# MLP down-projection of a two-block layer: a third pair by seven products, and half of the ordinary low parts made by ScalarE and an accumulating GpSimd transfer

## The chip, the core and the metric

The program runs on one core of one Trainium2 chip. The metric is device time in microseconds; the median of three runs is shown. The engines are named as in the profile: PE is TensorE's matrix multiplication and PEld its weight load, DVE is VectorE, ACT is ScalarE, POOL is GpSimd, SP is SyncE, which issues the loads.

## What is computed

The reference is a pair of transformer blocks on 256 tokens of width 2048. The first block ends with an MLP, and that is the part the change touches:

```python
u = jax.nn.relu(rms_norm(h, mlp_norm_g) @ w_up)      # 256 x 8192
h = h + (u * u) @ w_down                             # 8192 x 2048
```

All is float32. The projections before it (attention mixers) and the second block after it are left as they are.

## The kernel before

**Products in three terms.** Every float32 product is made of two `float32r` parts. The weights arrive from HBM as `raw`; ACT copies them to `w_high` (line 1274), which rounds; DVE makes `w_low = raw - w_high` (line 1593). The activations have a high and a low part too. PE adds high x high, high x low and low x high, so each product is three matmuls of 512 columns (lines 957, 958 and 959 in the quad jobs).

**Windows.** The weights of all projections come as one stream of 884 windows of 128 x 1024 (512 KB). There are `RAW_SLOTS` = 6 slots of `raw` and `AHEAD` = 5 slots of `w_high` and `w_low`. While PE works on window w, ACT and DVE split window w + 5. Every engine walks the same list (`walk`, line 552): window w, then the early stages of w, then the split of w + 5, then the late stages. ACT's split of s waits for the load of s and for `window_done` of s - 5, because its slot is still read until then. DVE's split waits for ACT's and for the same window. SP's `load(w)` (line 770) waits until the split of w - 6 has left its slot of `raw`. DVE counts its splits in `low_ready`, and PE waits for that count before each window.

**The MLP.** `plan_mlp` (line 344) runs four blocks of 2048 hidden features. A block has eight `features` jobs of four windows each (u = x W_up, transposed, with wide matmuls at line 970 and narrow ones at 982), then two `quads` jobs for W_down, each of which makes 1024 of the 2048 output columns; the fourth block has one quad job and two `tokens` jobs instead. That is seven quad jobs. A stage `u_square`, `u_split` squares and splits the hidden features of every second job (j = 0 to 3) into `actB`.

**A quad job** (`QuadJob`, line 87) goes through eight pairs of 128-row chunks in `QUAD_ORDER`. An "eight" pair takes two windows (side 0 and side 1), each with four products, 12 matmuls, so 24 in all. A "seven" pair multiplies its 2 x 2 blocks by Winograd's form of Strassen's scheme with seven products, 21 matmuls: its parts 0, 1 and 2 hold two products each (6 matmuls) and part 3 holds one (3 matmuls). Parts 0 and 1 are loaded; parts 2 and 3 hold sums of the weights that DVE makes in the free slots of `raw` (`sums_of`, lines 1603 to 1606). The matching sums of the activations ("forms") are made once per block by the stage `u_forms`: four sums on DVE, the high part on ACT (line 1476), the low part on DVE (line 1899). Before the change the sevens are pairs 0 and 1, so a quad job has 20 windows and 186 matmuls.

**Taking results away.** After the last seven, `add_sevens` (ACT line 1481, DVE lines 1912 to 1919) combines the seven products into H; after the job, `add_quads` (line 1929) adds the rest. The sevens use the banks of the other buffer, so a seven of one job waits for `add_quads` of the job before.

**GpSimd** makes only a few square roots by a power (lines 842, 846, 852) and issues no transfer. Below, k0, k1, ... are the windows of one quad job.

Of the kernel before, what the change touches and what calls it, by code (L numbers as in the profile page):

```python
# [16 lines left out]
P = 128  # L17
T = 256
# [490 lines left out]


SUMS = list(itertools.accumulate(int(part_of(w) == 1) for w in range(PLAN.windows)))

# [93 lines left out]
def build(nc, d, out):  # L606
    ctx = ExitStack()
    with ctx:
# [3 lines left out]
        def sem(name):  # L612
            return ctx.enter_context(nc.semaphore(name))
# [6 lines left out]
        act_high, act_low = ({n: act_both[n][:, :, part, :] for n in "AB"} for part in (0, 1))  # L620
        forms_both = sb("forms_both", [P, 2, 1024], F32R)
        H = sb("H", [P, TT, D])
# [68 lines left out]

        forms, forms_high, forms_low = m_slot(0), forms_both[:, 0, :], forms_both[:, 1, :]
        form_at = lambda f, p: slice(((f - 1) * 2 + SEVENS.index(p)) * P, ((f - 1) * 2 + SEVENS.index(p) + 1) * P)
        p1, u_one, u_two = slots[:, 4, 0:COLS], slots[:, 4, COLS:2 * COLS], slots[:, 5, 0:COLS]
# [26 lines left out]
        act_self, dve_self = sem("act_self"), sem("dve_self")  # L721
        sums_made = sem("sums_made")
        out_ready, half_done, wide_done = sem("out_ready"), sem("half_done"), sem("wide_done")
# [41 lines left out]
        def _(sp):  # L765
# [61 lines left out]
        def _(pool):  # L827
# [5 lines left out]
            def stage(w, name, *a):  # L833
# [13 lines left out]
                elif name in ("head_norm", "o_norm", "post_stat"):  # L847
# [5 lines left out]
                                            ALU.pow).then_inc(S["rstd"], 1)  # L853
            walk(n, lambda w: None, lambda w, s: None, stage)

        @block.tensor
        def _(pe):
# [65 lines left out]
            def products(w, tokens):  # L923
# [4 lines left out]
                if w > 0:  # L928
                    pe.wait_ge(low_ready, w + 1)
                for cc, c in enumerate(chunks_of(w)):  # L930
# [13 lines left out]
            def quads(w):  # L944
                job, k = WINDOW[w]
                first_of(w)
                pe.wait_ge(low_ready, w + 1)
                for x, (bank, (of, i, where), cc) in enumerate(job.products(k)):
                    cols = slice(cc * COLS, (cc + 1) * COLS)
                    if of == "u":  # L950
                        once("u_low", 4 * job.needs[1] + i // 4 + 1)
                        ah, al = (a["B"][:, i, where * P:(where + 1) * P] for a in (act_high, act_low))
                    else:
                        once("forms_low", job.needs[1] + 1)
                        ah, al = (a[:, form_at(i, where)] for a in (forms_high, forms_low))
# [19 lines left out]
            def narrow(w):  # L975
                job, k = WINDOW[w]
                ends = k == job.windows - 1
                pe.wait_ge(low_ready, w + 1)
                for cc, c in enumerate(chunks_of(w)):
# [266 lines left out]
        def _(act):  # L1246
# [8 lines left out]
            def split(w, s):  # L1255
# [12 lines left out]
                if s >= AHEAD and WINDOW[s - AHEAD][0].kind == "features":  # L1268
                    act.wait_ge(low_ready, s - AHEAD + 1)
                    act.wait_ge(wide_done, WIDE[s - AHEAD])  # L1270
                elif s >= AHEAD:
                    act.wait_ge(window_done, s - AHEAD + 1)
                cols = slice(0, COLS if part_of(s) == 3 else 2 * COLS)
                nc.scalar.activation(w_high[:, s % AHEAD, cols], raw[:, s % RAW_SLOTS, cols], ACT.Copy)\  # L1274
                    .then_inc(high_ready, 1)

            as_att = lambda: att[:, 2:4, :]

            def stage(w, name, *a):
# [193 lines left out]
                elif name == "u_forms":  # L1473
                    wait(act, n, "forms_made")
                    wait(act, n, "h_added", 0)
                    nc.scalar.activation(forms_high, forms, ACT.Copy).then_inc(S["forms_high"], 1)
                elif name == "add_sevens":
# [92 lines left out]
        def _(dve):  # L1570
# [8 lines left out]
            def split(w, s):  # L1579
                if s == 0:  # L1580
                    for half_, made, signal in ((slice(0, COLS), first_high, first_low),
# [14 lines left out]
            def sums_of(s):  # L1596
# [33 lines left out]
            def stage(w, name, *a):  # L1630
# [255 lines left out]
                elif name == "u_forms":  # L1886

                    wait(dve, n, "u_squared", 0)
                    wait(dve, n, "forms_high", 0)
                    u = a_slot(2).rearrange("p (q c x t) -> p q c x t", q=2, c=2, x=TT)  # L1890
                    a11, a12, a21, a22 = (u[:, :, c, x, :] for x, c in ((0, 0), (0, 1), (1, 0), (1, 1)))
                    s1, s2, s3, s4 = (forms[:, i * T:(i + 1) * T].rearrange("p (q t) -> p q t", q=2) for i in range(4))
                    done(nc.vector.tensor_tensor(s1, a21, a22, ALU.add))
# [4 lines left out]
                    wait(dve, n, "forms_high")  # L1898
                    nc.vector.tensor_tensor(forms_low, forms, forms_high.bitcast(F32), ALU.subtract)\
                        .then_inc(S["forms_low"], 1)  # L1900
# [269 lines left out]
```

## Time and profile before

| | us |
|---|---|
| median of 3 runs | 2503.59 (2503.17 to 2504.42) |
| span of the profiled execution | 2504.0 |
| PE busy | 2480.6 |
| DVE busy | 1753.6 |
| ACT busy | 1257.8 |
| POOL busy | 29.5 |

The profiled execution is given by its span alone, from its first instruction to its last; it lies 0.4 us above the median of the runs, so the span is taken as its time. Busy time counts the instructions' own durations. Matmuls overlap: a row of one 128 x 512 matmul reads 0.39 us, but the next one starts earlier than that, so the distance between starts is what counts. An instruction's idle time is followed by what released it.

### The profile page before, as it was taken

To read this page: it belongs to the slowest core of one execution; us is meant where nothing else is said; L and a number is where in the kernel's file an instruction comes from. 1 tells how busy PE (TensorE), PEld (TensorE's weight loads), DVE (VectorE), ACT (ScalarE), POOL (GpSimd) and SP (SyncE) were. 2 spreads that over 40 slices of the span, in tenths; PEclk is the share of its full clock that TensorE was granted. 3 is DMA by queue.
4 is the path that set the end of the run, shared out by engine and by line. 5 is a ranking of instruction groups with operands and counts; after the bars stand their busy time and mean duration, and the time that the engine had idled before them with its cause. 6 is when DMAs were issued, how large, how long until landed. Compare 5 with 4: busy or idle time off the path is not lost.

```text
span 2504.0 us, 38061 instructions
## 1 busy us (share of the span) xinstructions
PE 2480.6 (99%) x15416; PEld 2115.6 (84%) x15416; DVE 1753.6 (70%) x1978; ACT 1257.8 (50%) x1506; POOL 29.5 (1%) x26
## 2 busy tenths in 40 slices
PE   9999999999999999999999999999999999999998
PEld 7888888888888888888888888888888888888886
DVE  6656765668668677675777777775776666777777
ACT  7655344544444444445555555544654444444543
POOL 0000000000000000000000000000000000000000
PEclk9999999999999999999999999999999999999999
DMA  9454545546546546555545454556465565556553
GB/s 381 153 183 152 176 153 193 176 164 223 193 161 231 187 171 211 193 195 183 185 153 185 153 185 153 185 170 195 150 217 185 186 200 187 183 194 198 186 188 127
DMA packets 128239, 465.97 MB, mean 186 GB/s; under 512 B 14368, under 2 KB 14624, under 8 KB 127168
## 3 DMA queue, kind: packets, MB, share of 16 engines
q1 hardware_dynamic: 127920, 463.53, 55.2%
q8 instruction: 122, 2.00, 0.3%
q14 instruction: 53, 0.43, 0.1%
q10 hardware_dynamic: 144, 0.02, 0.0%
HBM read 461.39 MB, written 2.10 MB: 185 GB/s over the span
## 4 chain that ended last, share of the span: by engine, by line
PE 94%; issue 4%; DVE 2%; ACT 0%; DMA 0%; SPq 0%; DVEq 0%; POOL 0%; POOLq 0%
PE job L970 30%; PE job L982 16%; PE job L938 11%; PE job L940 11%; PE job L939 11%; PE job L957 2%; PE job L958 2%; PE job L959 2%; PE att L958 2%; PE att L957 2%; PE att L959 2%; PE att L1177 1%; PE att L998 0%; DVE w_low L1593 0%; PE att L1010 0%
## 5 line engine op out<-in xcount | busy, mean ns | idle before, releaser
L1274 ACT ACTIVATE w_high<-raw 128x1024 fp32r<-128x1024 f32 (+1 forms) x883 | 919.6, 1050 | 733.9 <-PE job L940 292.4
L1593 DVE TENSOR_TENSOR w_low<-raw,w_high 128x1024 fp32r<-128x1024 f32 (+1 forms) x883 | 1047.0, 1212 | 310.5 <-ACT w_high L1274 231.0
L970 PE MATMUL job<-actA,w_high 128*128 128x512 f32 x3328 | 798.3, 391 | 0.1
L970 PEld LDWEIGHTS job<-actA,w_high 128*128 128x128 f32 x3328 | 611.8, 188 | 119.9 <-issue 0.7
L982 PEld LDWEIGHTS job<-actA,w_low 128*128 128x128 f32 x3328 | 426.7, 191 | 16.2
L982 PE MATMUL job<-actA,w_low 128*128 128x256 f32 x3328 | 431.7, 283 | 0.0
L1796 DVE TENSOR_TENSOR slots<-job,slots 128x512 f32<-128x512 f32 x102 | 70.5, 691 | 344.1 <-ACT slots L1466 343.5
L938 PE MATMUL job<-w_high,actB 128*128 128x512 f32 x736 | 288.6, 392 | 2.5 <-DVE w_low L1593 2.0
L939 PE MATMUL job<-w_low,actB 128*128 128x512 f32 x736 | 287.1, 390 | 0.0
L940 PE MATMUL job<-w_high,actB 128*128 128x512 f32 x736 | 287.0, 390 | 0.0
L938 PE MATMUL job<-w_high,actA 128*128 128x512 f32 x576 | 230.9, 401 | 0.0
L940 PE MATMUL job<-w_high,actA 128*128 128x512 f32 x576 | 224.8, 390 | 0.0
L939 PE MATMUL job<-w_low,actA 128*128 128x512 f32 x576 | 224.6, 390 | 0.0
L1466 ACT ACTIVATE slots<-job 128x512 f32<-128x512 f32 x102 | 61.0, 598 | 240.6 <-PE job L982 240.6
L938 PEld LDWEIGHTS job<-w_high,actB 128*128 128x128 f32 x736 | 138.5, 188 | 32.2 <-DVE w_low L1593 2.4
L940 PEld LDWEIGHTS job<-w_high,actB 128*128 128x128 f32 x736 | 138.5, 188 | 28.9
L939 PEld LDWEIGHTS job<-w_low,actB 128*128 128x128 f32 x736 | 138.7, 188 | 28.1
L940 PEld LDWEIGHTS job<-w_high,actA 128*128 128x128 f32 x576 | 108.1, 188 | 23.4
L938 PEld LDWEIGHTS job<-w_high,actA 128*128 128x128 f32 x576 | 108.1, 188 | 22.7
L939 PEld LDWEIGHTS job<-w_low,actA 128*128 128x128 f32 x576 | 108.2, 188 | 21.1
L957 PE MATMUL job<-w_high,actB 128*128 128x512 f32 x210 | 82.2, 392 | 2.1 <-DVE w_low L1593 2.1
L958 PE MATMUL job<-w_low,actB 128*128 128x512 f32 x210 | 81.8, 390 | 0.0
(257 smaller groups left out, 1906.0 us busy)
## 6 DMA issues: line engine op xcount, KB each, us to landing
raw<-in_weights SPq DMA_DIRECT2D x855, 512.0 KB, 4.2
M<-in_mem_t SPq DMA_DIRECT2D x8, 256.0 KB, 8.0
slots<-in_mem SPq DMA_DIRECT2D x2, 1024.0 KB, 12.2
M<-in_x_t SPq DMA_DIRECT2D x4, 512.0 KB, 13.8
H<-in_x SPq DMA_DIRECT2D x2, 1024.0 KB, 9.0
out<-H SPq DMA_DIRECT2D x8, 256.0 KB, 3.2
slots<-in_w_small SPq DMA_DIRECT2D x1, 1024.0 KB, 9.7
slots<-in_post_mix_g SPq DMA_DIRECT2D x1, 1024.0 KB, 4.3
```

The costliest lines, as they stand in the source:

```text
L938: nc.tensor.matmul(to, ah, w_high[:, slot, cols], start=begins and cc == 0, stop=False)
L939: nc.tensor.matmul(to, ah, w_low[:, slot, cols], start=False, stop=False)
L940: mm = nc.tensor.matmul(to, al, w_high[:, slot, cols], start=False, stop=ends and cc == job.per - 1)
L957: nc.tensor.matmul(to, ah, w_high[:, w % AHEAD, cols], start=(k, x) in job.firsts, stop=False)
L958: nc.tensor.matmul(to, ah, w_low[:, w % AHEAD, cols], start=False, stop=False)
L959: mm = nc.tensor.matmul(to, al, w_high[:, w % AHEAD, cols], start=False, stop=(k, x) in job.lasts)
L970: mm = nc.tensor.matmul(J[job.buf][:, x, :], w_high[:, w % AHEAD, cols], act_both[job.act][:, c, :, :].rearrange("p a t -> p (a t)"), star ...
L982: mm = nc.tensor.matmul(J[job.buf][:, x, T:2 * T], w_low[:, w % AHEAD, cols], act_high[job.act][:, c, :], start=False, stop=ends and cc == ...
L1274: nc.scalar.activation(w_high[:, s % AHEAD, cols], raw[:, s % RAW_SLOTS, cols], ACT.Copy)\
L1466: nc.scalar.activation(by_feature(JOIN[to][:, half_ * COLS:(half_ + 1) * COLS]), J[buf][:, :, T:2 * T], ACT.Copy).then_inc(S["low_copied"], 1)
L1593: nc.vector.tensor_tensor(w_low[:, s % AHEAD, cols], raw[:, s % RAW_SLOTS, cols], w_high[:, s % AHEAD, cols].bitcast(F32), ALU.subtract).t ...
L1796: nc.vector.tensor_tensor(x, J[buf][:, :, 0:T], x, ALU.add).then_inc(S["joined"], 1)
```

## The change

The third seven: `QUAD_ORDER` makes pairs 0, 1 and 2 sevens, in another order. A quad job now has 22 windows: k0, k1 an eight, k2 to k5 a seven, k6, k7 an eight, k8 to k11 a seven, k12, k13 an eight, k14 to k17 a seven, and two eights in k18 to k21. `forms_both` grows from 1024 to 1536 columns, and `u_forms` runs for j = 0 (pairs 0 and 1, as before) and for j = 1 (pair 2, half the width).

The low parts: `by_transfer(w)` holds for side 1 of an eight whose slot was not used last by a `features` window. For such a window DVE makes no low part. ACT writes `-w_high` into the slot of `w_low` with a second copy of `raw` by -1, and POOL, which waits for that, issues a transfer of the same 512 KB of weights from HBM that is added to the slot. PE waits for the transfer's semaphore. It holds for k7, k13, k19 and k21 in every quad job, and for k1 too where the job before was a quad job: 4 x 4 + 3 x 5 = 31 transfers. All waits on `low_ready` are recounted, and SP and `sums_of` wait for ACT's second copy where there is no low part by DVE.

```diff
-QUAD_ORDER = (("eight", 2), ("seven", 0), ("eight", 3), ("eight", 4), ("seven", 1), ("eight", 5), ("eight", 6), ("eight", 7))
+QUAD_ORDER = (("eight", 3), ("seven", 0), ("eight", 4), ("seven", 1), ("eight", 5), ("seven", 2), ("eight", 6), ("eight", 7))
...
-            if j == 0:
-                p.put(job.end + 2, "u_forms", b)
+            if j < 2:
+                p.put(job.end + 2, "u_forms", j)
...
+def by_transfer(w):
+
+    job, k = WINDOW[w]
+    return (job.kind == "quads" and job.parts[k][0] == "eight" and job.parts[k][2] == 1
+            and WINDOW[w - AHEAD][0].kind != "features")
...
+        def low_wait(engine, w):
+
+            if by_transfer(w):
+                engine.wait_ge(low_landed[w % AHEAD], 16 * LANDED[w])
+            else:
+                engine.wait_ge(low_ready, LOWS[w])
+
+        def raw_wait(engine, w):
+
+            if by_transfer(w):
+                engine.wait_ge(neg_made, NEGS[w])
+            else:
+                engine.wait_ge(low_ready, LOWS[w])
...
-                    sp.wait_ge(low_ready, w - RAW_SLOTS + 1 + (part_of(w - RAW_SLOTS) == 0))
+                    raw_wait(sp, w - RAW_SLOTS + (part_of(w - RAW_SLOTS) == 0))
...
+            def split(w, s):
+
+                if by_transfer(s):
+                    pool.wait_ge(neg_made, NEGS[s])
+                    nc.gpsimd.dma_start(w_low[:, s % AHEAD, :], d["weights"][LOAD_AT[s] - 1], accum_op=ALU.add)\
+                        .then_inc(low_landed[s % AHEAD], 16)
+
+            walk(n, lambda w: None, split, stage)
...
                 nc.scalar.activation(w_high[:, s % AHEAD, cols], raw[:, s % RAW_SLOTS, cols], ACT.Copy)\
                     .then_inc(high_ready, 1)
+                if by_transfer(s):
+                    nc.scalar.activation(w_low[:, s % AHEAD, :], raw[:, s % RAW_SLOTS, :], ACT.Copy, scale=-1.0)\
+                        .then_inc(neg_made, 1)
...
+                if by_transfer(s):
+                    return
                 if part_of(s) == 1:
                     sums_of(s)
...
-                dve.wait_ge(low_ready, s + 3 - RAW_SLOTS)
+                raw_wait(dve, s + 1 - RAW_SLOTS)
+                raw_wait(dve, s + 2 - RAW_SLOTS)
```

## Rows read from the trace of the kernel before

**Rows 1.** The page: busy time of the engines, and the chain that ended last.
```profile
PE 2480.6 (99%) x15416; PEld 2115.6 (84%) x15416; DVE 1753.6 (70%) x1978; ACT 1257.8 (50%) x1506; POOL 29.5 (1%) x26
...
PE 94%; issue 4%; DVE 2%; ACT 0%; DMA 0%; SPq 0%; DVEq 0%; POOL 0%; POOLq 0%
```

**Rows 2.** Two stretches by windows: one quad job each, columns as headed.
```profile
core 0: us, PE busy (x) PEld busy (x) DVE busy (x) ACT busy (x) POOL busy (x), PEclk, DMA share, GB/s
...
550.71:594.30 43.59, 42.55 (x188) 34.57 (x186) 38.36 (x43) 21.54 (x23) 0.00 (x0) 1.00 0.54 193
...
594.30:636.60 42.30, 42.30 (x188) 35.05 (x187) 34.47 (x38) 21.46 (x22) 0.00 (x0) 1.00 0.64 224
```

**Rows 3.** Timeline of PE in the second quad job: start us, us, engine, line.
```profile
594.53 0.39 PE L957 MATMUL job<-w_high,actB 128*128 128x512 f32 x1
...
595.21 0.39 PE L957 MATMUL job<-w_high,actB 128*128 128x512 f32 x1
...
599.97 0.39 PE L957 MATMUL job<-w_high,actB 128*128 128x512 f32 x1
...
601.33 0.39 PE L957 MATMUL att<-w_high,forms_both 128*128 128x512 f32 x1
...
607.45 0.39 PE L957 MATMUL att<-w_high,actB 128*128 128x512 f32 x1
...
636.69 3.79 PE L970 MATMUL job<-actA,w_high 128*128 128x512 f32 x16
```

**Rows 4.** Waits of the whole span: who for whom, us, times, longest.
```profile
PEld job L957 <- DVE w_low L1593: 7.5, 8, 1.0
...
PE job L957 <- DVE w_low L1593: 4.1, 8, 0.5
```

**Rows 5.** Timeline of the first quad job: start us, us, engine, line.
```profile
558.40 1.06 ACT L1471 ACTIVATE actB<-slots 128x1024 fp32r<-128x1024 f32 x1 [0.96 <-DVE slots L1878]
...
558.67 0.39 PE L959 MATMUL att<-w_high,forms_both 128*128 128x512 f32 x1
...
559.37 5.02 ACT L1274 ACTIVATE w_high<-raw 128x1024 fp32r<-128x1024 f32 x5
...
559.56 0.50 PE L957 MATMUL job<-w_high,forms_both 128*128 128x512 f32 x1 [0.51 <-DVE w_low L1593]
...
561.16 5.76 DVE L1593 TENSOR_TENSOR w_low<-raw,w_high 128x1024 fp32r<-128x1024 f32 x5
...
562.43 0.50 PE L957 MATMUL job<-w_high,actB 128*128 128x512 f32 x1 [0.53 <-DVE w_low L1593]
```

**Rows 6.** Timeline of ACT in the second quad job: start us, us, engine, line.
```profile
601.59 1.06 ACT L1274 ACTIVATE w_high<-raw 128x1024 fp32r<-128x1024 f32 x1 [0.30 <-PE job L959]
...
602.95 1.06 ACT L1274 ACTIVATE w_high<-raw 128x1024 fp32r<-128x1024 f32 x1 [0.30 <-PE att L959]
...
604.30 2.01 ACT L1274 ACTIVATE w_high<-raw 128x1024 fp32r<-128x1024 f32 x2 [0.30 <-PE att L959]
```

**Rows 7.** Line 776 from 550 to 637 us: issues on SP, and to landing.
```profile
L776 SPq DMA_DIRECT2D raw<-in_weights x36: 327/328/433, 557.3 to 636.6; - x36
...
DMA to landing us min/median/max: 3.1/4.5/6.8
```

**Rows 8.** Line 852: duration ns min/median/max of a POOL instruction.
```profile
L852 POOL TENSOR_TENSOR rstd<-msq,half x13: 695/1637/2552, 60.4 to 1755.7; 128x8 f32<-128x8 f32 x12, 128x2 f32<-128x2 f32 x1
```

**Rows 9.** The page: GB/s that the DMA engines moved, 40 slices.
```profile
GB/s 381 153 183 152 176 153 193 176 164 223 193 161 231 187 171 211 193 195 183 185 153 185 153 185 153 185 170 195 150 217 185 186 200 187 183 194 198 186 188 127
```

**Rows 10.** Groups of DVE, 540 to 1125 us: busy us, mean ns, idle.
```profile
L1593 DVE TENSOR_TENSOR w_low<-raw,w_high 128x1024 fp32r<-128x1024 f32 x229 | 272.7, 1221 | 56.1 <-ACT w_high L1274 36.7 <-PE job L982 15.4
...
L1604 DVE TENSOR_TENSOR raw<-raw 128x512 f32<-128x512 f32 x14 | 9.7, 692 | 0.5
...
L1899 DVE TENSOR_TENSOR forms_both<-M,forms_both 128x1024 fp32r<-128x1024 f32 x3 | 3.7, 1225 | 3.6 <-ACT forms_both L1476 3.6
```

**Rows 11.** Wait of ACT for the forms, 480 to 550 us.
```profile
ACT forms_both L1476 <- DVE M L1896: 3.1, 1, 3.1
```

More of the change, by code:

```diff
@@ L508, in part_of @@
     return job.parts[k][2] if job.kind == "quads" and job.parts[k][0] == "seven" else None
+def by_transfer(w):
+    job, k = WINDOW[w]
+    return (job.kind == "quads" and job.parts[k][0] == "eight" and job.parts[k][2] == 1
+            and WINDOW[w - AHEAD][0].kind != "features")
+LOWS = list(itertools.accumulate(int(not by_transfer(w)) for w in range(PLAN.windows)))
+NEGS = list(itertools.accumulate(int(by_transfer(w)) for w in range(PLAN.windows)))
+LANDED = [sum(by_transfer(v) for v in range(w % AHEAD, w + 1, AHEAD)) for w in range(PLAN.windows)]
 SUMS = list(itertools.accumulate(int(part_of(w) == 1) for w in range(PLAN.windows)))
@@ L620, in build @@
         act_high, act_low = ({n: act_both[n][:, :, part, :] for n in "AB"} for part in (0, 1))
-        forms_both = sb("forms_both", [P, 2, 1024], F32R)
+        forms_both = sb("forms_both", [P, 2, 1536], F32R)
         H = sb("H", [P, TT, D])
@@ L690, in build, with form_at @@
         post_g = a2(6)
-        forms, forms_high, forms_low = m_slot(0), forms_both[:, 0, :], forms_both[:, 1, :]
-        form_at = lambda f, p: slice(((f - 1) * 2 + SEVENS.index(p)) * P, ((f - 1) * 2 + SEVENS.index(p) + 1) * P)
+        forms, forms_high, forms_low = Mf[:, 0:1536], forms_both[:, 0, :], forms_both[:, 1, :]
+        form_cols = lambda j: slice(0, 1024) if j == 0 else slice(1024, 1536)
+        def form_at(f, p):
+            at = (f - 1) * 2 * P + SEVENS.index(p) * P if p < 2 else 1024 + (f - 1) * P
+            return slice(at, at + P)
         p1, u_one, u_two = slots[:, 4, 0:COLS], slots[:, 4, COLS:2 * COLS], slots[:, 5, 0:COLS]
@@ L722, in build @@
         sums_made = sem("sums_made")
+        neg_made, low_landed = sem("neg_made"), [sem(f"low_landed{i}") for i in range(AHEAD)]
         out_ready, half_done, wide_done = sem("out_ready"), sem("half_done"), sem("wide_done")
@@ L928, in products @@
                 if w > 0:
-                    pe.wait_ge(low_ready, w + 1)
+                    low_wait(pe, w)
                 for cc, c in enumerate(chunks_of(w)):
@@ L946, in quads @@
                 first_of(w)
-                pe.wait_ge(low_ready, w + 1)
+                low_wait(pe, w)
                 for x, (bank, (of, i, where), cc) in enumerate(job.products(k)):
@@ L953, in quads @@
                     else:
-                        once("forms_low", job.needs[1] + 1)
+                        once("forms_low", 2 * job.needs[1] + (1 if where < 2 else 2))
                         ah, al = (a[:, form_at(i, where)] for a in (forms_high, forms_low))
@@ L977, in narrow @@
                 ends = k == job.windows - 1
-                pe.wait_ge(low_ready, w + 1)
+                low_wait(pe, w)
                 for cc, c in enumerate(chunks_of(w)):
@@ L1268, in split @@
                 if s >= AHEAD and WINDOW[s - AHEAD][0].kind == "features":
-                    act.wait_ge(low_ready, s - AHEAD + 1)
+                    act.wait_ge(low_ready, LOWS[s - AHEAD])
                     act.wait_ge(wide_done, WIDE[s - AHEAD])
@@ L1475, in stage @@
                     wait(act, n, "h_added", 0)
-                    nc.scalar.activation(forms_high, forms, ACT.Copy).then_inc(S["forms_high"], 1)
+                    cols = form_cols(a[0])
+                    nc.scalar.activation(forms_high[:, cols], forms[:, cols], ACT.Copy).then_inc(S["forms_high"], 1)
                 elif name == "add_sevens":
@@ L1889, in stage @@
                     wait(dve, n, "forms_high", 0)
-                    u = a_slot(2).rearrange("p (q c x t) -> p q c x t", q=2, c=2, x=TT)
+                    j, pairs = a[0], 2 - a[0]
+                    u = a_slot(2 + j).rearrange("p (q c x t) -> p q c x t", q=2, c=2, x=TT)[:, 0:pairs]
                     a11, a12, a21, a22 = (u[:, :, c, x, :] for x, c in ((0, 0), (0, 1), (1, 0), (1, 1)))
-                    s1, s2, s3, s4 = (forms[:, i * T:(i + 1) * T].rearrange("p (q t) -> p q t", q=2) for i in range(4))
+                    s1, s2, s3, s4 = (forms[:, form_cols(j)].rearrange("p (f q t) -> p f q t", f=4, q=pairs)[:, f]
+                                      for f in range(4))
                     done(nc.vector.tensor_tensor(s1, a21, a22, ALU.add))
@@ L1898, in stage @@
                     wait(dve, n, "forms_high")
-                    nc.vector.tensor_tensor(forms_low, forms, forms_high.bitcast(F32), ALU.subtract)\
+                    cols = form_cols(j)
+                    nc.vector.tensor_tensor(forms_low[:, cols], forms[:, cols], forms_high[:, cols].bitcast(F32),
+                                            ALU.subtract)\
                         .then_inc(S["forms_low"], 1)
```

1 line of the change is left out of this document (removed).

## The prediction

> **What bounds the kernel now.** I read the page first. PE is busy 99% of the span and holds 94% of the chain that ended last, so time falls only where PE has less to do or waits less, and it rises with every wait put before a matmul [rows 1]. Next, the windows of two quad jobs. In the second PE is busy all 42.30 us; in the first 42.55 of 43.59. DVE is busy 38.36 and 34.47 us there, near its limit, while ACT has half its time free (21.5 us busy) and POOL is idle [rows 2]. The third view is PE's timeline. Three matmuls take 595.21 - 594.53 = 0.68 us, 0.227 us each; the whole job goes from 594.53 to 636.69, 42.16 us, which is 186 x 0.227 [rows 3]. So a full window is 2.72 us, parts 0 to 2 of a seven 1.36 us, part 3 0.68 us. The waits come last: DVE's low part is late eight times in the span [rows 4], two each in the four quad jobs that follow features. One is 559.56 - 558.67 - 0.227 = 0.66 us [rows 5]; eight make 5.3 us.
>
> **The change part by part.** *The third seven.* It replaces 24 matmuls by 21 in seven jobs: 21 x 0.227 = 4.8 us off PE, all on the path. This is the whole gain that arithmetic gives, 0.19% of the span.
>
> *DVE.* An eight costs it two low parts, 2 x 1.22 = 2.4 us; a seven three and a half of them and four sums of 0.69 us, 3.5 x 1.22 + 4 x 0.69 = 7.0 us [rows 10]. The third seven adds 4.6 us a job; the four or five low parts given away take 4.9 to 6.1 off. If DVE kept them, a first job would want 43.0 us of DVE in about as much of PE; so it keeps its load of today. Giving them away removes a wait that the third seven would bring, and none that is there now: the two late low parts of a first job hang on `u_square` and `u_split`, which stay in their place ahead of k4 and k6. I take zero, and 5.3 us as the most that could come.
>
> *The forms.* The second `u_forms` is half as wide as the first, whose four sums keep ACT waiting 3.1 us [rows 11] before ACT's copy of 1.06 us and DVE's low part of 1.22 us [rows 10]; at most 5.4 us in each of four blocks. It stands in the features jobs, where the first one makes PE wait for nothing: none of PE's waits for DVE names it [rows 4]. Cost zero; with no cover at all it would be 4 x 5.4 = 22 us.
>
> *The deadline of the sums.* The second seven now starts at k8, right after a seven and one eight. Counted from the start of k4, DVE gets there by ACT's copy (0.26 + 1.06), the low part of k8 (1.22), four sums (2.8), a copy and a low part (2.5): 7.8 us. PE is at k9 after 1.36 + 0.68 + 2.72 + 2.72 + 1.36 = 8.84 us. The slack is 1.0 us (4.4 before). The loads of k14 and k15 wait for the low part of k9 and land at about the time they are needed; a load at the slow end of 6.8 us [rows 7] would be late by some 1.2 us. I take zero, because a stall at k7 or k13, below, gives just this slack back; the bound is 2 x 7 x 1.2 = 17 us.
>
> *The traffic.* Each job has 16 loads as before, and five transfers more, whose bytes are read from HBM and whose target is read too. By bytes this is at most 5 x 2 x 0.524 MB in 42 us, 125 GB/s on top of 224 [rows 2]; together 349, and the first slice shows 381 [rows 9]. So bandwidth does not stop it, but loads and transfers share the same engines and stretch each other.
>
> *The transfer, on which it all hangs.* ACT's copy of a window begins 0.26 us after PE starts the window that follows the freeing one, because it needs `window_done`. In the second job k3 starts at 601.33 and ACT copies k7 from 601.59 [rows 3, 6]. Two copies back to back take 2.01 us [rows 6], so -w_high stands at 603.60. PE wants k7 at 607.45 [rows 3]. **The transfer has 3.85 us** from POOL's wait to its semaphore. For k13 and k19 the four windows between are the same (1.36 + 1.36 + 0.68 + 2.72 = 6.12 us), so is the allowance. For k21 the windows between are 8.84 us long, which gives 6.6 us plus the stall of k19, and for k1 four full ones, 10.9 us, which gives 8.6; these two I cost at nothing, whatever the latency below.
>
> In the four jobs after features k7 is tighter. ACT waits there until 558.40 for `u_split` and then copies k6, k7, ... from 559.37, 1.0 us each [rows 5]; the third copy in this chain would be -w_high of k7, done at 562.41. PE wants k7 at 562.43 + 2.72 = 565.15 [rows 5]: 2.74 us.
>
> Let L be the time from POOL's release to landing. PE stalls L - 3.85 at 17 places (three in each of seven jobs, less the four) and L - 2.74 at four: together 21 L - 76.4 us, as long as L is over 3.85. A stall is not made good later: the next deadline is counted from PE's own windows, which move along. With the 4.8 us off, the change costs **21 L - 81.2 us**; it breaks even at L = 3.87 us and is slower by 0.2% (5 us, about what a measurement here can tell) at 4.1 us.
>
> No accumulating transfer and none issued by POOL is in this trace. The nearest rows are SP's loads of the same 512 KB in this stage: 3.1 us at the least, 4.5 the median, 6.8 the most, and 0.33 us of issuing [rows 7]. The low end is L = 3.1, where adding and POOL's issuing cost nothing. For the high end I add to the slowest load a second pass for reading the target, 0.524 MB at 381 GB/s = 1.4 us, and POOL's slowest instruction, 2.55 us [rows 8]: 10.8 us. I take the median load and one second pass, 4.5 + 1.4 = **5.9 us**, nearest to the middle row because the transfer meets a load in flight most of the time (36 loads of 4.5 us in 79 us). The stalls are then 17 x 2.05 + 4 x 3.16 = 47.5 us.
>
> The Trainium skill, page "DMA: Bandwidth & Descriptors", section "Anatomy of one DMA", puts a GpSimd-issued transfer at about 2.0 us plus bytes over 436 GB/s. By that estimate L is 3.2 us, only k7 of the first jobs is late (4 x 0.46), and the sum would be 2504.0 - 4.8 + 1.8 = 2501.0 us; it prices no adding and no other traffic, and no row here has such a transfer.
>
> **Sum.** 2504.0 - 4.8 + 47.5 = 2546.7 us on the profiled execution. Its span is 0.4 us above the median, so against the median of the runs 2546.3; I say 2546.
>
> **The rivals.** *The transfer fits (20%).* Place: between ACT's second copy and PE's wait before k7, k13 and k19. If adding is done in the stream and costs no second pass, and POOL issues as fast as SP, L is near the 3.1 us of the fastest load, 17 stalls vanish and four of 0.36 us stay: 2504.0 - 4.8 + 1.4 - 0.4 = 2500 us, not slower. It decides from L below 3.87, and stays within 0.2% up to 4.1. For it: the loads of 3.1 us. Against it: half of all loads already take over 4.5.
>
> *No second pass, but the crowd (10%).* L = 4.5: 21 x 4.5 - 81.2 = 13 us, 2517 us.
>
> *A slow issue (18%).* POOL writes out its transfer in software and takes as long as its slowest instruction, 2.55 us, on top of 5.9: L = 8.4, 21 x 8.4 - 81.2 = 95 us, 2599 us. For it: POOL's eight columns take 1.64 us in the median [rows 8]. Or POOL has to wait out a low part of DVE, 1.22 us, when it wants the memory port: L = 7.1, 2572 us. The Trainium skill, page "SBUF — State Buffer", section "Who interferes with whom", says that a DVE instruction with two SBUF inputs holds up only GpSimd's reads; by this rule the latter does not happen. No run shows it yet.
>
> *The late low parts vanish too (6%).* If DVE's relief reached k4 and k6 of the first jobs and the transfers fit, 2504.0 - 4.8 - 5.3 - 0.4 = 2493.5 us. Against it: those low parts are late behind work that the change leaves in place.
>
> **How the numbers follow.** The forecast, L between 4.9 and 6.9, gets 46%, and 2546 is its value. Slower by over 0.2%: 46 + 10 + 18 = 74%; within 0.2%: 20%; faster: 6%. The range goes from 2500 (the transfer fits) to 2594 (L = 8.2, the slowest load with a second pass: 21 x 8.2 - 81.2 = 91 us, less the 0.4); it leaves out the 6% below and about half of the slow case above.
>
> **What would show it.** Right: PE has 15395 matmuls, 21 fewer. In the chain and the waits, PE waits for a transfer into `w_low` 21 times, some 2 us each at k13 and k19, some 3 us at k7 of the first jobs; ACT has 31 copies by -1, DVE 24 fewer 1024-column low parts (31 given away, 14 fewer eights' and 21 more sevens') and 28 more sums; from POOL's issue to landing the median is near 5.9 us. At k1 and k21 there is no wait. Wrong: a median under 4 us with a PE that never waits for it, or waits that name DVE's low parts at k9 and k15, which would mean that the sums and not the transfers are late.

## The result, and the profile after

The change makes the kernel slower: 2645.13 us, median of five runs (2643.86 to 2646.54), against 2503.75 us for the kernel before in the same session. The ratio is 1.0563, with a 95% interval of 1.0551 to 1.0576. I had forecast 2546 us, with a range up to 2594: the direction was right, the size was not, by 99 us, and the time lies 51 us outside the range. In the table of experiments one of four runs of transfers_only is left out: it took 3103.9 us at a granted clock of 0.749, in a slow state of the chip.

The page of the kernel after, from its parts 1, 2 (TensorE's granted clock), 4, 5 and 6; it answers to [rows 1]:

```profile
span 2643.2 us, 38150 instructions
PE 2529.9 (96%) x15395; PEld 2145.4 (81%) x15395; DVE 1756.5 (66%) x2009; ACT 1296.5 (49%) x1555; POOL 56.8 (2%) x57
PEclk9999999988998898898999999999999999999999
PE 87%; DMA 6%; issue 3%; ACT 2%; DVE 0%; SPq 0%; DVEq 0%; POOL 0%; ACTq 0%; POOLq 0%
L995 PE MATMUL att<-w_high,actB 128*128 128x512 f32 x140 | 76.5, 546 | 90.1 <-DMA w_low<-in_weights 90.1
w_low<-in_weights POOLq DMA_DIRECT2D x31, 512.0 KB, 7.8
```

The granted clock on the page of the kernel before:

```profile
PEclk9999999999999999999999999999999999999999
```

Two things are new. The chain that ended last now has a DMA in it, 6% of the span, and its group says which: the transfer into `w_low`. And in the row of the clock, slices 9 to 19 read 8 in seven places, where before every slice read 9. The quad jobs lie there. PE's busy time also rose, by 49.3 us, although it has 21 matmuls less; an engine that does less work in more busy time is working more slowly. The mean of L995's `att` matmuls, 546 ns where one of these takes 390 otherwise, says the same.

The waits of the kernel after for the new transfer, over the whole span, then DVE's late low parts from 540 to 1300 us, and POOL's issues with the time from issue to landing; they answer to [rows 4, 7]:

```profile
PEld att L995 <- DMA w_low<-in_weights: 99.0, 21, 5.8
PE att L995 <- DMA w_low<-in_weights: 90.1, 21, 5.4
...
PE job L995 <- DVE w_low L1637: 4.2, 8, 0.5
...
L889 POOL DMA_DIRECT2D w_low<-in_weights x31: 872/872/1063, 560.9 to 1242.9; - x31
...
DMA to landing us min/median/max: 6.4/7.8/10.6
```

PE waits at the 21 places foretold and nowhere else for a transfer. DVE's eight late low parts are there as before. But a transfer takes 7.8 us in the median, not 5.9.

The timeline of the kernel after, from ACT's copy to the end of the first late window, k7 of the first quad job; it answers to [rows 5]:

```profile
559.55 1.04 ACT L1315 ACTIVATE w_low<-raw 128x1024 fp32r<-128x1024 f32 x1
560.91 1.06 POOL L889 DMA_DIRECT2D w_low<-in_weights  x1 [91.58 <-ACT w_low L1315]
563.34 0.39 PE L997 MATMUL job<-w_high,actB 128*128 128x512 f32 x1
569.13 0.79 PE L995 MATMUL att<-w_high,actB 128*128 128x512 f32 x1 [5.40 <-DMA w_low<-in_weights]
569.73 0.63 PE L996 MATMUL att<-w_low,actB 128*128 128x512 f32 x1
570.15 0.63 PE L997 MATMUL att<-w_high,actB 128*128 128x512 f32 x1
...
573.90 0.39 PE L997 MATMUL att<-w_high,actB 128*128 128x512 f32 x1
```

The same stretch by windows (us, PE, PEld, DVE, ACT and POOL busy with their counts, granted clock, DMA share, GB/s):

```profile
564.00:570.00 6.00, 0.87 (x2) 0.77 (x3) 4.38 (x6) 2.52 (x3) 0.00 (x0) 0.75 0.90 213
570.00:574.00 4.00, 4.00 (x11) 3.08 (x11) 0.00 (x0) 0.00 (x0) 0.00 (x0) 0.53 0.43 170
574.00:578.00 4.00, 4.00 (x20) 3.29 (x19) 1.22 (x1) 3.30 (x4) 0.00 (x0) 1.00 0.11 15
```

PE idles 5.40 us. Then matmuls start 0.427 us apart, not 0.227: the granted clock is 0.53, close to the half that is the 1.2 GHz level, while PE is busy all the time. At 573.9 it is back at 2.4 GHz. From 569.13 to 573.90 there are 11 starts in 4.77 us; at full clock they take 2.50. So this one wait costs 5.40 us, and 2.27 us more behind it.

**Where the 139.2 us of span went** (2643.2 - 2504.0). The 21 matmuls give back 4.8. The waits are 90.1, and each costs 0.16 more from start to start, because a row's 0.39 us ends later than the next matmul would have begun (0.39 - 0.227): 93.5 together. That leaves 139.2 + 4.8 - 93.5 = 50.5 us, 2.4 for each wait. I also added up, from the starts of the matmuls after each wait, what they take over 0.227 us apiece: 52 us, 1.7 to 3.0 behind each of the 21. The slow clock is the rest. (In runs the difference is 141.4; the other 2 us are that the page of before lay 0.4 us above its median, while this span lies 1.9 below.)

The fall doesn't always come at once. A later wait of the kernel after:

```profile
630.71 0.50 PE L995 MATMUL att<-w_high,actB 128*128 128x512 f32 x1 [4.19 <-DMA w_low<-in_weights]
631.05 0.40 PE L996 MATMUL att<-w_low,actB 128*128 128x512 f32 x1
...
632.12 0.63 PE L997 MATMUL att<-w_high,actB 128*128 128x512 f32 x1
```

Here PE works over a microsecond at full clock before it slows down. Someone who looks only at the first matmul after a wait misses it.

### The profile page after: what moved, and what is told of

Read it like the earlier page. It is cut to its first block, busy times and chain, and to the rows that moved or that the text cites. A ratio compares the mean times of both kernels' runs of the same rounds, so it can differ in the third digit from the quotient of the medians.

```text
span 2643.2 us, 38150 instructions
## 1 busy us (share of the span) xinstructions
PE 2529.9 (96%) x15395; PEld 2145.4 (81%) x15395; DVE 1756.5 (66%) x2009; ACT 1296.5 (49%) x1555; POOL 56.8 (2%) x57
## 4 chain that ended last, share of the span: by engine, by line
PE 87%; DMA 6%; issue 3%; ACT 2%; DVE 0%; SPq 0%; DVEq 0%; POOL 0%; ACTq 0%; POOLq 0%
PE job L1008 29%; PE job L1020 15%; PE job L976 11%; PE job L978 10%; PE job L977 10%; DMA w_low<-in_weights 6%; PE att L995 2%; PE att L996 2%; PE att L997 2%; ACT w_high L1312 1%; PE job L995 1%; PE job L996 1%; PE job L997 1%; ACT w_low L1315 1%; PE att L1215 1%
## 5 line engine op out<-in xcount | busy, mean ns | idle before, releaser
L1637 DVE TENSOR_TENSOR w_low<-raw,w_high 128x1024 fp32r<-128x1024 f32 (+1 forms) x866 | 1024.6, 1208 | 445.0 <-ACT w_high L1312 370.3
L976 PE MATMUL job<-w_high,actB 128*128 128x512 f32 x736 | 287.9, 391 | 2.3 <-DVE w_low L1637 1.5
L977 PE MATMUL job<-w_low,actB 128*128 128x512 f32 x736 | 286.6, 389 | 0.0
L978 PE MATMUL job<-w_high,actB 128*128 128x512 f32 x736 | 286.4, 389 | 0.0
L995 PE MATMUL att<-w_high,actB 128*128 128x512 f32 x140 | 76.5, 546 | 90.1 <-DMA w_low<-in_weights 90.1
L995 PEld LDWEIGHTS att<-w_high,actB 128*128 128x128 f32 x140 | 36.3, 260 | 107.0 <-DMA w_low<-in_weights 99.0
## 6 DMA issues: line engine op xcount, KB each, us to landing
slots<-in_w_small SPq DMA_DIRECT2D x1, 1024.0 KB, 10.4
```

The costliest lines, as they stand in the source:

```text
L976: nc.tensor.matmul(to, ah, w_high[:, slot, cols], start=begins and cc == 0, stop=False)
L977: nc.tensor.matmul(to, ah, w_low[:, slot, cols], start=False, stop=False)
L978: mm = nc.tensor.matmul(to, al, w_high[:, slot, cols], start=False, stop=ends and cc == job.per - 1)
L995: nc.tensor.matmul(to, ah, w_high[:, w % AHEAD, cols], start=(k, x) in job.firsts, stop=False)
L1637: nc.vector.tensor_tensor(w_low[:, s % AHEAD, cols], raw[:, s % RAW_SLOTS, cols], w_high[:, s % AHEAD, cols].bitcast(F32), ALU.subtract).t ...
```

## Experiments

**What is to be told apart.** My theory now: the latency of the transfer sets the 21 waits, and each wait then costs a stretch at half clock. Rivals: the third seven or its forms cost PE something of their own; the slow matmuls come from something else, such as the transfers' traffic; and the latency is made by adding, by POOL's issuing, by bytes or by the loads beside it.

| kernel | median us (runs) | ratio to before, 95% | granted clock |
|---|---|---|---|
| after | 2645.13 (5) | 1.0563 [1.0551, 1.0576] | 0.972 |
| sevens_only | 2522.33 (5) | 1.0077 [1.0064, 1.0090] | 0.995 |
| transfers_only | 2579.26 (3) | 1.0293 [1.0277, 1.0309] | 0.990 |
| wait_filled | 2599.68 (4) | 1.0383 [1.0367, 1.0399] | 0.997 |
| high_first | 2589.25 (4) | 1.0340 [1.0324, 1.0356] | 0.986 |
| plain_from_pool | 2587.53 (1) | - | 0.987 |
| half_transfer | 2594.04 (1) | - | 0.985 |
| thin_loads | 2583.08 (1) | - | 0.985 |
| before_high_first | 2497.84 (9) | 0.9975 [0.9966, 0.9985] | 0.997 |
| long_lead_high_first | 2526.12 (4) | 1.0087 [1.0073, 1.0101] | 0.996 |
| one_lead_high_first | 2519.52 (5) | 1.0062 [1.0049, 1.0074] | 0.995 |
| sevens_high_first | 2522.39 (5) | 1.0073 [1.0060, 1.0087] | 0.993 |
| later_first_seven | 2513.48 (5) | 1.0039 [1.0026, 1.0053] | 0.997 |

Kernels with one run are compared by their profiles, and their time only roughly. These three leave out part of the low parts or of the weights, so their results are wrong; they serve to measure times alone.

### The two halves of the change: sevens_only, transfers_only

```diff
# sevens_only, in by_transfer: DVE makes every low part
-            and WINDOW[w - AHEAD][0].kind != "features")
+            and WINDOW[w - AHEAD][0].kind != "features" and False)
# transfers_only: two sevens, the order of before
-QUAD_ORDER = (("eight", 3), ("seven", 0), ("eight", 4), ("seven", 1), ("eight", 5), ("seven", 2), ("eight", 6), ("eight", 7))
+QUAD_ORDER = (("eight", 2), ("seven", 0), ("eight", 3), ("eight", 4), ("seven", 1), ("eight", 5), ("eight", 6), ("eight", 7))
```

> The change with no transfer at all: three sevens in the new order, every low part by DVE. If the whole loss of the change lies in the transfers (my theory: 21 waits of 4 to 6 us and the slower clock after each), this is near 2504 - 4.8 = 2499 us, 2498 to 2508 with a late low part here and there. Rival, the third seven needs the relief (DVE has 43.0 us of work in 43.1 us of PE, and the second and third seven leave 1.0 us for their sums): then PE waits for DVE at k9 and k15, by 1 to 3 us each, and the time is 2510 to 2540 us.

> The change with the order of before: two sevens, transfers kept. They now fall on k1 (second jobs), k7, k9, k15, k17 and k19. Between a window five back and its use lie 6.12 us at k7 and k15, but 8.84 us at k9 and k17 and 10.9 us at k19. My theory (the stall is the latency less the room the windows leave) expects waits at k7 and k15 only, 14 of them, of 4 to 6 us, some 1.3 us or less at k9 and k17, and about 2504 + 14 x (4.3 + 2.2) = 2595 us. Rival (any transfer stalls PE, because POOL, the queue or the port is the trouble): waits at all of k7, k9, k15, k17, k19, and over 2640 us.

Waits of sevens_only, 540 to 1300 us, and `add_quads` and two matmuls at its longest wait:

```profile
PE job L995 <- DVE H L1978: 11.2, 3, 4.1
PE job L995 <- DVE w_low L1637: 5.3, 9, 1.1
...
601.21 1.40 DVE L1978 SCALAR_TENSOR_TENSOR H<-job,rstd,H 128x512 f32<-128x512 f32 x2
602.53 1.40 DVE L1978 SCALAR_TENSOR_TENSOR H<-att,rstd,H 128x512 f32<-128x512 f32 x2
603.98 0.80 PE L995 MATMUL job<-w_high,actB 128*128 128x512 f32 x1 [4.10 <-DVE H L1978]
604.58 0.63 PE L996 MATMUL job<-w_low,actB 128*128 128x512 f32 x1
```

The third seven alone makes the kernel 18 us slower although it has 21 matmuls less. The time is the rival's, the place is neither's: at k9 and k15 PE waits next to nothing. It waits at k2 of three second jobs for `add_quads` of the job before (line 1978), and these waits too are followed by slow matmuls (some 1.7 us lost behind each). The third seven ends four windows before the end of the job instead of six, so `add_sevens`, some 6 us of DVE, is done later, the low parts and sums stand behind it, and `add_quads` behind them. In the kernel after this wait is absent. The low parts given away have made room on DVE, but PE's own stalls, 13 us a job, also give DVE time, and this run does not part the two. Whatever share is the transfers', they cost more than it.

Waits of transfers_only over the whole span:

```profile
PE att L995 <- DMA w_low<-in_weights: 47.2, 17, 4.6
```

It waits at k7 and k15 of the seven jobs (14) and a little at three k9. The places are those of my theory, and not the rival's; the time is 16 us under the 2595 us foretold, because the seven waits at k7 are 1.7 to 2.7 us long instead of 4 to 6. Its clock is 0.990: the third seven isn't needed for the slow stretches. Waits of 0.8 to 1.8 us were followed by less than 0.2 us of loss, those of 3.9 to 4.6 us by 1.6 to 3.0 (from the starts of the matmuls, as above); between them it varied. A wait of 1.94 us was followed by 1.7 us of loss, one of 3.56 us by 0.1.

### The clock: wait_filled, high_first

```diff
# wait_filled: four matmuls of zeros, added to the bank in use, ahead of the wait
+                if by_transfer(w) and k in (7, 13, 19):
+                    pe.wait_ge(zeros_set, 1)
+                    for _ in range(4):
+                        nc.tensor.matmul(quad_bank(job.buf, ("C", 1, 0)), zeros[:, 0:P], zeros,
+                                         start=False, stop=False)
                 low_wait(pe, w)
```

> The change, with four float32 matmuls of zeros (128 x 512, added to a bank of the job, which they leave as it is) put ahead of PE's wait at k7, k13 and k19. The transfers and their latency are as in the change. Theory: the clock falls because PE stands still for about 4 us, and that costs 2.4 us after each of 21 waits, 50 us in all. With the wait filled the granted clock stays at 1.0 and the time is about 2643 - 50 = 2593 us, a little more where the zeros run past the landing. Rival: the clock falls for another reason, and the time stays at 2645 us with rows of 0.63 us after the wait.

Windows of wait_filled, the first two of the stretch shown above, and its timeline there (the profile has two records for each of the four float32 matmuls of zeros, hence x8):

```profile
564.00:570.00 6.00, 3.73 (x10) 1.62 (x9) 4.42 (x6) 2.52 (x3) 0.00 (x0) 1.00 0.89 212
570.00:574.00 4.00, 4.00 (x19) 3.25 (x19) 0.29 (x1) 1.09 (x2) 0.00 (x0) 1.00 0.42 171
...
563.62 3.60 PE L989 MATMUL att<-slots 128*128 128x512 f32 x8
569.48 0.50 PE L1001 MATMUL att<-w_high,actB 128*128 128x512 f32 x1 [2.27 <-DMA w_low<-in_weights]
569.81 0.40 PE L1002 MATMUL att<-w_low,actB 128*128 128x512 f32 x1
```

This run settles what makes the matmuls slow. The first late window begins at 569.48 (569.13 in the kernel after), so the transfer is no earlier; the DMA engines are as busy (0.89 and 0.90, then 0.42 and 0.43). Only PE's idle time is cut, from 5.40 to 2.27 us, by work that is worth nothing. The clock stays at 1.00, 19 matmuls start in the next 4 us instead of 11, and the span is 47.3 us shorter. That is nearly the 50 us from above, found by another way. The traffic of the transfers is not the cause.

```diff
# high_first: in a transfer's window the terms with w_high come before the wait
-                low_wait(pe, w)
+                later, high_first = [], by_transfer(w)
+                if high_first:
+                    pe.wait_ge(high_ready, w + 1)
+                else:
+                    low_wait(pe, w)
...
+                    if high_first:
+                        nc.tensor.matmul(to, al, w_high[:, w % AHEAD, cols], start=False, stop=False)
+                        later.append((to, ah, cols, (k, x) in job.lasts))
+                        continue
...
+                if high_first:
+                    low_wait(pe, w)
+                    for to, ah, cols, last in later:
+                        mm = nc.tensor.matmul(to, ah, w_low[:, w % AHEAD, cols], start=False, stop=last)
```

> The change, but in a window that takes its low part from a transfer PE first does the eight matmuls that need w_high alone and waits for the transfer only then. 8 x 0.227 = 1.8 us of each wait is covered: 21 x 1.8 = 38 us less, 2607 us, if the clock falls after a wait of 2.5 to 4 us as after one of 4.3 to 5.8. If the shorter waits leave the clock at its upper level, another 21 x 2.2 = 46 us comes back: 2561 us.

Waits of high_first, 540 to 1300 us:

```profile
PE att L1009 <- DMA w_low<-in_weights: 56.5, 20, 4.3
```

Eight of the twelve matmuls of a window can run before its low part is needed: 1.8 us more of allowance. The waits fall by 90.1 - 56.5 = 33.6 us, and the time by 56: the other 22 us are clock. The result lies between the two times foretold, since the shorter waits (1.6 to 4.3 us) leave the clock up in some places and not in others.

### The latency: plain_from_pool, half_transfer, thin_loads

```diff
# plain_from_pool
-                    nc.gpsimd.dma_start(w_low[:, s % AHEAD, :], d["weights"][LOAD_AT[s] - 1], accum_op=ALU.add)\
+                    nc.gpsimd.dma_start(w_low[:, s % AHEAD, :], d["weights"][LOAD_AT[s] - 1])\
# half_transfer
+                    nc.gpsimd.dma_start(w_low[:, s % AHEAD, 0:COLS], d["weights"][LOAD_AT[s] - 1][:, 0:COLS], accum_op=ALU.add)\
# thin_loads: SP loads 128 of 1024 columns in the quad jobs
+                part = slice(0, COLS // 4 if WINDOW[w][0].kind == "quads" else 2 * COLS)
```

> The change with the transfer writing instead of adding; the low parts of these 31 windows are then the weights themselves. If adding costs a second pass of 1.4 us, issue to landing falls from a median of 7.8 to about 6.4 us and the time by 21 x 1.4 = 29 us to 2616. If POOL's own issuing is what is slow, the latency stays at 7.8 and the time at 2645. If adding is the whole difference to a load, the latency is 4.5 us and the time about 2645 - 21 x 3.3 - 46 = 2530.

> The change with transfers of the first 512 columns only (256 KB); the other half of these low parts is left at minus w_high. If the latency goes with the bytes (adding and traffic), it falls from 7.8 to about 6.4 us or less and the waits by 21 x 1.4 = 29 us. If it is a fixed cost of POOL's issuing and of completing, it stays at 7.3 us or more and the time changes by under 10 us.

> The change with the quad jobs' own loads cut to the first 128 of 1024 columns (the rest of those weights is left as it was in the slot); the transfers stay whole. If the crowd of loads is what stretches a transfer, the median from issue to landing falls from 7.8 to about 5.5 us or less, and the time by some 21 x 2.3 us and part of the clock's 50 us, to 2560 us or under. If POOL's issuing and adding are slow by themselves, it stays at 7 us or more and the time above 2620 us.

The tile `w_low` on POOL, in plain_from_pool (with the landing of SP's loads there, 550 to 640 us, as the third line), then half_transfer, thin_loads and one_lead_high_first (below), one fence each:

```profile
L889 POOL DMA_DIRECT2D w_low<-in_weights x31: 537/537/712, 560.0 to 1188.9; - x31
...
DMA to landing us min/median/max: 3.6/6.2/7.6
...
DMA to landing us min/median/max: 3.2/4.2/7.1
```

```profile
DMA to landing us min/median/max: 4.0/6.2/8.3
```

```profile
DMA to landing us min/median/max: 5.2/5.5/9.5
```

```profile
L889 POOL DMA_DIRECT2D w_low<-in_weights x3: 866/869/1051, 590.1 to 952.5; - x3
...
DMA to landing us min/median/max: 5.3/5.4/5.5
```

Out of 7.8 us, adding makes 1.6 (7.8 against 6.2 for the same bytes without it), of which 0.33 is the issue itself (0.87 against 0.54 us; SP needs 0.33). Half the bytes save 1.6. The loads beside it make 2.3: with an eighth of their bytes the median is 5.5 (the 9.5 us are at the ends of the jobs, where whole loads for the next job come in). The three transfers of one_lead_high_first, at 5.4, agree with that, because they too have few loads beside them. The windows from issue to landing of one of these, and of a transfer of the kernel after that also has no other transfer near it (columns as above):

```profile
590.11:595.61 5.50, 4.86 (x22) 3.69 (x21) 5.43 (x8) 0.64 (x1) 1.05 (x1) 1.00 0.62 125
578.07:585.59 7.52, 3.71 (x17) 2.74 (x15) 5.65 (x7) 3.16 (x4) 0.88 (x1) 0.89 0.82 200
```

The bytes beside a transfer are not the whole of it, though. In transfers_only the seven transfers at k7 land in 5.3 to 5.5 us with whole loads in flight, while the other transfers of that kernel take 6.7 to 10.4; which loads stretch a transfer that meets them, no run took apart. The waits follow the latency: 57.4, 61.8 and 52.4 us in 21 places in these kernels, 90.1 in the kernel after, and each time falls further than the waits do, for part of the slow stretches goes too. So the sums in the three expectations above came out too high for plain_from_pool (2616 against 2588) and too low for thin_loads (2560 against 2583).

So a transfer of 512 KB that adds takes some 5.4 us with the loads out of its way. The Trainium skill, page "DMA: Bandwidth & Descriptors", section "Anatomy of one DMA — SWDGE (gpsimd) path", gives a fit from which I had estimated 3.2 us; that fit has no term for adding and none for other traffic, and the measurement decides. The plain transfers' fastest, 3.6 us, comes near to it.

### A better form? before_high_first, sevens_high_first, long_lead_high_first, one_lead_high_first, later_first_seven

before_high_first is the kernel before with the order of high_first in every quad window (`high_first = True`). The next three are the kernel after with it, and with these transfers: none; those with a long lead (k1, k21); that of k1 alone. later_first_seven has no transfers, and its second jobs begin with two eights:

```diff
# long_lead_high_first; one_lead_high_first has "and k == 1" in its place
-            and WINDOW[w - AHEAD][0].kind != "features")
+            and k in (1, 21) and WINDOW[w - AHEAD][0].kind != "features")
# later_first_seven
+SECOND_ORDER = (("eight", 3), ("eight", 4), ("seven", 0), ("eight", 5), ("seven", 1), ("seven", 2), ("eight", 6), ("eight", 7))
```

> The kernel before, but in every window of the quad jobs PE does the matmuls that need w_high alone first and waits for the low part only then. Theory: the eight late low parts of 0.66 us are covered by eight or four matmuls, 5.3 us less: 2498.5 us. Rival: in these windows the high part is as late, or the wait moves on to the next window: 2503.5 us, no change.

> Three sevens, no transfer, high parts first in the quad windows. Against three sevens alone (2522 us) the small waits for low parts (about 7 us on PE) are covered; the three waits for add_quads (11.2 us) and the clock after them stay, since they come from DVE's own queue. Theory: 2522 - 9 = 2513 us, slower than before, so that a third seven costs more on DVE than its 4.8 us on PE. Rival: with the windows overlapping more, DVE catches up and the time is under 2500 us.

> Three sevens; transfers only where the windows leave them 8.84 us or more (k21 in each job, k1 in second jobs: 10 in all); high parts first in every quad window. Theory: with a lead of 6.6 + 1.8 us and more no transfer is waited for, DVE is relieved just where add_quads was late with all low parts on DVE, and the time is 2504 - 4.8 - 5.3 = 2494 us, faster than both. Rival: with k7, k13 and k19 back on DVE it is over its limit again, and low parts at k9 to k15 or add_quads are late: 2505 to 2520 us.

> As three sevens with long leads and high parts first (2526 us), but with transfers at k1 of the second jobs alone, three in all. The seven waits at k21 (16.4 us on PE) and their clock go; DVE gets seven low parts back, 1.2 us each, of which those ahead of add_quads are late. Theory: no wait for a transfer, and between 2498 and 2512 us. Rival: without k21's relief DVE falls back as far as without any transfer, and the time is that of three sevens with high parts first.

> As three sevens with high parts first (2522 us), but in the three second jobs of a block the first seven starts at k4 instead of k2, and the other two follow each other (k10 to k17). What is late in that kernel is add_quads of the job before, three times 4.3 to 5.3 us, and the clock after it, since the first seven of the second job writes into that job's banks. Theory: PE then needs it 5.4 us later, the three waits vanish with their 4.9 us of slow matmuls, and the time is 2520.1 - 15.6 - 4.9 = 2500 us or less: the third seven pays if DVE's queue is given room, though hardly more than high parts first alone (2497.8 us). Rival: DVE has too much to do whatever the order, and the wait comes back at the two sevens in a row: 2505 to 2520 us.

Windows of before_high_first, the first quad job; it answers to [rows 2]:

```profile
549.96:593.00 43.04, 43.04 (x192) 35.65 (x191) 38.87 (x44) 22.96 (x24) 0.00 (x0) 1.00 0.56 195
```

**It beats both kernels**: 2497.84 us, 6 us under the kernel before. The eight waits for DVE's low parts are gone from its list of waits, and PE is busy all of the job. The eight had cost 4.1 us of waiting and 8 x 0.16: 5.4 us. It needs no third seven, no transfer and no work less. This is what was foretold for it (2498.5 us).

Waits of PE in sevens_high_first, one_lead_high_first, long_lead_high_first (with ACT's copy of k21 in its first quad job) and later_first_seven (with its longest wait), 540 to 1300 us, one fence each:

```profile
PE job L999 <- DVE H L1990: 14.1, 3, 5.3
```

```profile
PE job L999 <- DVE H L1990: 11.6, 3, 4.2
```

```profile
PE att L1009 <- DMA w_low<-in_weights: 13.5, 7, 3.7
PE job L999 <- DVE H L1990: 4.9, 3, 2.2
...
584.86 1.06 ACT L1324 ACTIVATE w_high<-raw 128x1024 fp32r<-128x1024 f32 x1 [0.93 <-DMA raw<-in_weights]
```

```profile
PE att L1000 <- ACT w_high L1325: 9.5, 7, 2.5
...
622.24 0.76 PE L1000 MATMUL att<-w_high,forms_both 128*128 128x512 f32 x1 [2.47 <-ACT w_high L1325]
```

With a third seven, one late thing takes the place of another. Without transfers it is `add_quads` (14.1 us). One transfer a second job takes 2.5 us off that. The transfers at k1 and k21 take 9.2 off, but k21 is itself late in all seven jobs. The stalls at k19 no longer push it back, and ACT's copy of k21 now waits for its load: of the 8.4 us of allowance that I had reckoned with, 4.6 to 7.7 were left, and the transfers landed 7.2 to 9.4 us after their release. Two eights at the start of the second jobs remove the wait for `add_quads` wholly, but then two sevens stand in a row, and the copy of the second one's sums is late by 2.4 to 2.5 us in each of the three second jobs; the other four waits of that row, 0.55 us each, are in the first jobs, and the three kernels above have them too. In these four kernels the time that I had as theory was missed each time, by 8 to 32 us (2513, 2498 to 2512, 2494 and 2500 us against 2522, 2520, 2526 and 2513); the rivals for one_lead_high_first and later_first_seven, that DVE falls back and that the wait returns at the two sevens in a row, came true. The third seven's 4.8 us were not earned in any form that I ran; whether another order would earn them stays open. A low part loaded plainly by ACT's queue was not tried.

## Why the prediction was wrong

**Right.** The direction: slower. The 15395 matmuls and no wait at k1 or k21. The places: 21 waits, and their form: stall = L - 3.85 or L - 2.74. With the measured 7.8 these give 3.95 and 5.06; measured were 3.7 to 4.6 at the 17 and 5.2 to 5.4 at the four. The formula 21 L - 76.4 gives 87.4 us of waiting at L = 7.8; 90.1 were measured. L was to count from POOL's release, which lies 0.3 us before the issue (559.55 + 1.04 against 560.91 in the first late window); so counted it is 8.1 in the mean, and the formula gives 93.7 against the 93.5 from start to start. The sums kept their deadline at k9 and k15, also in sevens_only, where no stall helps them, and the forms held up nobody, both costed at nothing. DVE's eight late low parts stayed (4.2 us). A stall was not made good later.

**Wrong, first: the term L.** I took 5.9 us, "the median load and one second pass". It measured 7.8, so the stalls came to 90.1 instead of 47.5. The row that I started from, SP's load, was the right neighbour but an incomplete one. Adding costs 1.6 (I had 1.4), but a transfer issued by POOL is slower than SP's load even without it: plain, it takes 6.2, against 4.2 for the loads in the same kernel and stretch, and 4.5 for those of before. (The loads that fly beside a lone plain transfer take about 6 us too, as those issued at 573.89 and 612.78 us do, so part of it may lie in the meeting of the two.) I had set this difference to zero in the forecast and made a rival of it. "A slow issue" had 2.55 us for it and L = 8.4. The plain issue takes only 0.54 us, 0.21 over SP's, so most of the difference lies after it; what it is there, no run took apart. Its second form, a wait for DVE's memory port, has no support: DVE was busy 5.43 of 5.50 us beside the first of the three transfers of one_lead_high_first, and all three landed within 5.3 to 5.5 us. The rule of the Trainium skill, page "SBUF — State Buffer", section "Who interferes with whom", cited against it in the prediction, fits that.

**Wrong, second: a term that wasn't there.** "21 L - 81.2" lets a stall cost its own length. Each cost some 2.4 us more, in PE's half clock behind it: 50 us of the 99 by which I missed. The term L makes 40, the 0.3 us between release and issue 6, and the difference of span and median the last 2. The quad jobs of before have only PE waits of 0.5 us or less, and there I had looked. But the kernel before has one long wait elsewhere, in its second block, and its trace would have given the term. Timeline of PE in the kernel before, and its windows there (columns as above):

```profile
1757.56 3.50 PE L998 MATMUL att<-ident,H 128*128 128x128 f32 x16 [3.78 <-DVE H L1985]
...
1753.00:1757.00 4.00, 0.78 (x4) 0.32 (x2) 1.38 (x5) 1.37 (x4) 0.69 (x1) 1.00 0.59 204
1757.00:1761.00 4.00, 3.44 (x17) 3.47 (x18) 4.00 (x11) 2.29 (x6) 0.00 (x0) 0.57 0.00 0
1761.00:1765.00 4.00, 4.00 (x22) 3.20 (x21) 4.00 (x10) 3.03 (x10) 0.00 (x0) 1.00 0.00 0
```

Behind a wait of 3.78 us the clock is 0.57 for 4 us, then 1.00. At half speed that is a loss of up to 4 x 0.43 = 1.7 us for a wait; 21 of them are 36 us. With it the forecast would have been 2582 us, and with the measured L as well 2622. By L alone the result would have been 2504.0 + 82.6 = 2587 us, inside the range. The Trainium skill, page "TensorE: Matmul & The Clock Gate", section "HAM oscillation — how this bites in real kernels", tells of a kernel in which every wait for a transfer lets the clock fall, so that each step starts slow; the granted clock of 0.53 behind PE's idle time is the same picture here, though in the experiments not every wait let it fall.

**Wrong, third, and without effect on the sum:** "Giving them away removes a wait that the third seven would bring" names a wait that exists, though how much of its removal is due to the low parts given away is not shown; and I looked for it at the low parts. It is `add_quads`, which the prediction doesn't name; sevens_only shows it at 11.2 us in three places. Had DVE had less relief, this could have been one more place of loss.

## What to carry to other kernels

Before a low part or any other operand is moved from an engine to a transfer, count the time from the release of its buffer to its use, and ask for a margin over the transfer's latency in the traffic of that stage, issue by that queue and adding included. A wait of several microseconds on a PE that was at full clock must be priced at its length and the slow stretch behind it (in these kernels always from 3.6 us on, sometimes between 1.8 and 3.6); look for the longest PE wait anywhere in the trace of before, and at the clock behind it. In products of several terms, issue first those whose operands are ready first: here this gained 6 us for nothing, and 33.6 us of waiting where the operand was very late.

## What the runs showed of the hardware that I had not expected

PE comes out of a wait at full clock and falls afterwards, as at 632.12 us, or is already at half, as at 569.13; either way 1.7 to 3.0 us are lost. Four matmuls of zeros ahead of the wait kept the clock at 1.00 and gave back 47 us. An issue by POOL took 0.87 us when it adds and 0.54 when it doesn't, against 0.33 by SP, and halving the bytes of an adding transfer saved only 1.6 of 7.8 us. The adding transfer took 5.4 us with few loads beside it and 7.8 in the median among them, and DVE was the busier beside the faster one (5.43 of 5.50 us against 5.65 of 7.52).
